# Modulation vectors: full-precision matmuls tile by tile, or split float32r tiles four at a time

## What is computed

```python
sil_c = jax.nn.silu(c)
sil_cc = jax.nn.silu(c_ctx)
mx = (sil_c @ w_ada[l] + b_ada[l])[:, None, :]      # w_ada[l]: 1024 x 6144, float32
mc = sil_cc @ w_ada[l] + b_ada[l]
xsh1, xsc1, xg1, xsh2, xsc2, xg2 = jnp.split(mx, 6, axis=-1)
csh1, csc1, cg1, csh2, csc2, cg2 = jnp.split(mc, 6, axis=-1)
px = _split_in(_modulate(x, xsh1, xsc1) @ w_in[l])  # _modulate: x * (1 + scale) + shift
pc = _split_in(_modulate(ctx, csh1, csc1) @ w_in[l])
```

## Time and profile before

| what | us |
|---|---|
| median of 3 runs (4956.92 to 4962.1) | 4957.29 |
| the profiled execution | 4959.43 |
| its span in the trace | 4957.7 |
| TensorE busy, whole span | 4444.5 |
| VectorE busy | 2856.5 |
| ScalarE busy | 1816.6 |
| modulation matmuls (line 676), 768 records, busy | 88.9 |
| first row copied (line 657) | 25.77 |
| last row copied | 103.15 |
| bias added (line 692) | 107.02 |
| first matmul of the mixers | 133.67 |

### The profile page before, as it was taken

The page is one execution under the profiler, slowest core; times in us unless marked ns, Lnnn a source line. Parts: engine busy times, 40 slices in busy tenths (PEclk is TensorE's granted clock), DMA queues, the critical chain, the costliest instruction groups (busy, mean ns, idle before and its releaser), DMA issues. The chain is left out here.

```text
span 4957.7 us, 59869 instructions
## 1 busy us (share of the span) xinstructions
PE 4444.5 (90%) x22171; PEld 3705.2 (75%) x22171; DVE 2856.5 (58%) x5083; ACT 1816.6 (37%) x2570; POOL 413.2 (8%) x308
## 2 busy tenths in 40 slices
PE   7888888877998556999999996999999999899998
PEld 5777775654874355999999995776878877677887
DVE  1577776775445987888888885334343333344332
ACT  1546554333321033333333332346233233643322
POOL 0000000000001611222222220000000000000000
PEclk9899999998999788999999998999999999999999
DMA  6111111102321025878787782211323322122232
GB/s 247 64 39 35 39 35 34 47 17 70 91 93 49 22 102 222 281 269 281 270 279 274 276 279 80 73 56 39 98 90 98 96 75 68 41 72 92 94 96 83
DMA packets 195952, 578.14 MB, mean 117 GB/s; under 512 B 17328, under 2 KB 66736, under 8 KB 194352
## 3 DMA queue, kind: packets, MB, share of 16 engines
q1 hardware_dynamic: 157888, 433.77, 25.9%
q0 software_dynamic: 36864, 134.23, 8.0%
q10 hardware_dynamic: 1008, 7.55, 0.4%
HBM read 548.22 MB, written 27.26 MB: 116 GB/s over the span
## 5 line engine op out<-in xcount | busy, mean ns | idle before, releaser
L402 DVE TENSOR_TENSOR tile_rest<-tile_raw,tile_up 128x1024 fp32r<-128x1024 f32 (+2 forms) x288 | 338.5, 1180 | 782.2 <-ACT tile_up L393 782.1
L410 PE MATMUL layer_psum<-hn_up,tile_up 128*128 128x512 f32 x1344 | 534.8, 398 | 20.8 <-DVE hn_rest L497 20.8
L411 PE MATMUL layer_psum<-hn_up,tile_rest 128*128 128x512 f32 x1344 | 527.1, 392 | 0.0
L412 PE MATMUL layer_psum<-hn_rest,tile_up 128*128 128x512 f32 x1344 | 526.8, 392 | 0.0
L393 ACT ACTIVATE tile_up<-tile_raw 128x1024 fp32r<-128x1024 f32 (+2 forms) x288 | 291.5, 1018 | 369.0 <-PE layer_psum L412 368.2
L2159 PE MATMUL ex_psum<-ex_t_up,ex_u_up 128*128 128x384 f32 x1024 | 344.2, 336 | 11.3 <-ACT ex_prod L2233 6.6
L2177 PE MATMUL ex_psum<-ex_prod_up,ex_v_up 128*128 128x384 f32 x1024 | 342.8, 335 | 2.3 <-DVE xT L2299 2.3
L2160 PE MATMUL ex_psum<-ex_t_up,ex_u_rest 128*128 128x384 f32 x1024 | 343.8, 336 | 0.0
L2161 PE MATMUL ex_psum<-ex_t_rest,ex_u_up 128*128 128x384 f32 x1024 | 343.7, 336 | 0.0
L2179 PE MATMUL ex_psum<-ex_prod_rest,ex_v_up 128*128 128x384 f32 x1024 | 342.7, 335 | 0.0
L2178 PE MATMUL ex_psum<-ex_prod_up,ex_v_rest 128*128 128x384 f32 x1024 | 342.6, 335 | 0.0
(11 more groups left out here) (440 smaller groups left out, 10145.2 us busy)
## 6 DMA issues: line engine op xcount, KB each, us to landing
ex_u<-in_peer_u SPq DMA_DIRECT2D x128, 512.0 KB, 6.5
tT<-in_peer_v SPq DMA_DIRECT2D x128, 512.0 KB, 7.0
tile_raw<-in_w_gu SPq DMA_DIRECT2D x88, 512.0 KB, 3.6
xT<-in_w_head SPq DMA_DIRECT2D x56, 512.0 KB, 3.6
mod_w<-in_w_ada SPq DMA_DIRECT2D x48, 512.0 KB, 4.7
mg_w_raw<-in_w_merge SPq DMA_DIRECT2D x48, 512.0 KB, 3.6
expert_table<-et_rows SPq DMA_DIRECT2D x6, 4096.0 KB, 11.8
ex_rows<-expert_table SPq DMA_DIRECT2D x64, 384.0 KB, 7.9
```

The lines of the kernel that those rows point to most:

```text
L402: self.nc.vector.tensor_tensor(out=self.rest[:, n % self.SLOTS, 0:blocks, :], in0=self.raw[n % self.RAWS][:, 0:blocks, :], in1=self.up[:, ...
L410: self.nc.tensor.matmul(dst, w_up, up, start=first, stop=False)
L411: self.nc.tensor.matmul(dst, w_rest, up, start=False, stop=False)
L412: return self.nc.tensor.matmul(dst, w_up, rest, start=False, stop=last)
```

## The change

The matmuls of the stage are made in float32r with split operands, on four tiles at once. `sil` is cut in two parts that stand beside each other as four stationary columns (`both`: columns 0 and 1 the rounded part, 2 and 3 the remainder). Each weight tile is cut too: ScalarE copies the loaded tile `raw` to `up` (line 678 of the new kernel), VectorE writes `raw - up` to `w_rest` (723). There are six `raw` buffers and two sets of `up` and `w_rest`, a set being four tiles; the `w_rest` sets lie in the still unused `mem.x_up` and `mem.x_rest`. For each of the twelve groups of four tiles TensorE makes 16 matmuls of 512 moving columns: for each d one against `up` and one against `w_rest` (705, 706). A result has four rows, the parts of the two vectors, and two adds on VectorE (730, 731) bring them together. ScalarE copies a group's rows (670) into one of two small row buffers, and TensorE transposes them in fours (694) one group behind instead of all 48 at the end. A load buffer is free again when VectorE has cut its tile. TensorE waits for all of ScalarE's loads at its start. The loops over six columns of tiles are written out.

```diff
+    GROUP = 4
+    GROUPS = 6 * DB // GROUP
+    RAWS = 6
...
         def _(sp):
-            with sp.Fori(0, 6) as i:
-                for k in range(8):
-                    load_tile(sp, w, 0, k, i, io["w_ada"][i, k])
+            for n in range(GROUPS * GROUP):
+                if n >= RAWS:
+                    sp.wait_ge(w_cut, START + n - RAWS + 1)
+                sp.dma_start(raw[n % RAWS][:], io["w_ada"][n // 8, n % 8]).then_inc(landed[n % RAWS], 16)
...
-            with act.Fori(0, 6) as i:
-                for half in range(2):
-                    act.wait_ge(w.filled, w.fill_at(0, (half + 1) * PER_BANK - 1, i))
-                    nc.scalar.activation(rows[:, bass.ds(i * D + half * 512, 512)], B[half][0:2, :],
-                                         ACT.Copy).then_inc(row_out, 1)
+            act.wait_ge(sil_ready, START + 1)
+            nc.scalar.activation(both[:, :, 0:2], sil[:], ACT.Copy).then_inc(sil_up_ready, 1)
+
+            def row(g):
+                act.wait_ge(filled, START + g + 1)
+                if g >= 2:
+                    act.wait_ge(turned, START + g - 1)
+                nc.scalar.activation(rows[:, g % 2, :], B[g % 2][0:4, :], ACT.Copy).then_inc(row_out, 1)
+
+            for g in range(GROUPS):
+                for k in range(GROUP):
+                    n = g * GROUP + k
+                    act.wait_ge(landed[n % RAWS], START + 16 * (n // RAWS + 1))
+                    if g >= 2:
+                        act.wait_ge(filled, START + g - 1)
+                    nc.scalar.activation(up[g % 2][:, k, :, :], raw[n % RAWS][:], ACT.Copy).then_inc(w_up_ready, 1)
+                    if k == 1 and g > 0:
+                        row(g - 1)
+            row(GROUPS - 1)
...
-                    for d in range(DB):
-                        last = nc.tensor.matmul(B[half][0:2, at * P:(at + 1) * P], sil[:, d, :], w.ring[k][:, d, :],
-                                                start=d == 0, stop=d == DB - 1)
-                    last.then_inc(w.filled, 1)
...
+            def turn(g):
+                pe.wait_ge(row_out, START + g + 1)
+                for k in range(GROUP):
+                    m = g * GROUP + k
+                    last = nc.tensor.transpose(B[2][:, 4 * m:4 * m + 4], rows[:, g % 2, k * P:(k + 1) * P],
+                                               mem.c("ident")[0:4, 0:4])
+                last.then_inc(turned, 1)
+
+            pe.wait_ge(sil_cut, START + 1)
             pe.wait_ge(x_loaded, START + 64)
...
+            for g in range(GROUPS):
+                pe.wait_ge(w_cut, START + (g + 1) * GROUP)
+                if g >= 2:
+                    pe.wait_ge(row_out, START + g - 1)
+                for d in range(DB):
+                    nc.tensor.matmul(B[g % 2][0:4, :], both[:, d, :], up[g % 2][:, :, d, :], start=d == 0, stop=False)
+                    last = nc.tensor.matmul(B[g % 2][0:4, :], both[:, d, :], w_rest[g % 2][:, :, d, :], start=False,
+                                            stop=d == DB - 1)
+                last.then_inc(filled, 1)
+                if g > 0:
+                    turn(g - 1)
+            turn(GROUPS - 1)
...
+            for n in range(GROUPS * GROUP):
+                g, k = n // GROUP, n % GROUP
+                dve.wait_ge(w_up_ready, START + n + 1)
+                if g >= 2:
+                    dve.wait_ge(filled, START + g - 1)
+                nc.vector.tensor_tensor(out=w_rest[g % 2][:, k, :, :], in0=raw[n % RAWS][:],
+                                        in1=up[g % 2][:, k, :, :].bitcast(F32), op=ALU.subtract).then_inc(w_cut, 1)
...
+            seq(nc.vector.tensor_tensor(out=mem.mod[:], in0=sums[:, :, 0, :], in1=bias, op=ALU.add))
+            seq(nc.vector.tensor_tensor(out=mem.mod[:], in0=sums[:, :, 1, :], in1=mem.mod[:], op=ALU.add))
```

More of the change, by code:

```diff
@@ L620, in phase_modulation @@
 def phase_modulation(nc, io, mem):
-    PER_BANK = 512 // P
+    GROUP = 4
+    GROUPS = 6 * DB // GROUP
+    RAWS = 6
     with Phase(nc, "mod") as ph:
-        w = ph.stream(8, [(6, 8, list(range(8)))])
         B = ph.banks()
         cond, sil = ph.sb("cond", [P, DB, 2]), ph.sb("sil", [P, DB, 2])
+        both = ph.sb("both", [P, DB, 4], F32R)
+        raw = [ph.sb(f"raw{n}", [P, DB, P]) for n in range(RAWS)]
+        up = [ph.sb(f"up{g}", [P, GROUP, DB, P], F32R) for g in range(2)]
+        w_rest = [t[:].rearrange("p d t -> p (d t)").rearrange("p (k d n) -> p k d n", k=GROUP, d=DB)
+                for t in (mem.x_up, mem.x_rest)]
         masks = ph.sb("masks", [P, N_MASKS, P])
-        rows = ph.sb("rows", [2, 6 * D])
+        rows = ph.sb("rows", [4, 2, GROUP * P])
+        landed = [ph.sem(f"landed{n}") for n in range(RAWS)]
+        w_up_ready, w_cut, filled = ph.sem("w_up_ready"), ph.sem("w_cut"), ph.sem("filled")
+        sil_up_ready, sil_cut = ph.sem("sil_up_ready"), ph.sem("sil_cut")
         x, cm = mem.attT, mem.convT[:, 0:4, :].rearrange("p b t -> p (b t)").rearrange("p (d c) -> p d c", c=C)
@@ L634, in phase_modulation @@
         order, modulated, up_ready, cut = ph.sem("order"), ph.sem("modulated"), ph.sem("up_ready"), ph.sem("cut")
-        w.credited.append(row_out)
-        block = ph.block(w)
+        block = ph.block()
         @block.sync
         def _(sp):
-            with sp.Fori(0, 6) as i:
-                for k in range(8):
-                    load_tile(sp, w, 0, k, i, io["w_ada"][i, k])
+            for n in range(GROUPS * GROUP):
+                if n >= RAWS:
+                    sp.wait_ge(w_cut, START + n - RAWS + 1)
+                sp.dma_start(raw[n % RAWS][:], io["w_ada"][n // 8, n % 8]).then_inc(landed[n % RAWS], 16)
         @block.scalar
@@ L679, in _ @@
-            pe.wait_ge(row_out, START + CREDIT + 12)
-            pe.wait_ge(x_loaded, START + 64)
[L681 to L684, removed]
+            def turn(g):
[5 more added lines that the diff above has]
+                last.then_inc(turned, 1)
@@ L686, in _ @@
+            turn(GROUPS - 1)
         @block.vector
         def _(dve):
+            dve.wait_ge(sil_up_ready, START + 1)
+            nc.vector.tensor_tensor(out=both[:, :, 2:4], in0=sil[:], in1=both[:, :, 0:2].bitcast(F32),
+                                    op=ALU.subtract).then_inc(sil_cut, 1)
+            for n in range(GROUPS * GROUP):
[5 more added lines that the diff above has]
+                                        in1=up[g % 2][:, k, :, :].bitcast(F32), op=ALU.subtract).then_inc(w_cut, 1)
@@ L688, in _ @@
             seq = Order(dve, order)
-            seq.body(0, 2)
-            dve.wait_ge(turned, START + 1)
+            seq.body(0, 3)
+            dve.wait_ge(turned, START + GROUPS)
             bias = mem.par[:, PARAM_AT["b_ada"]].unsqueeze(2).to_broadcast([P, 48, 2])
-            seq(nc.vector.tensor_tensor(out=mem.mod[:], in0=B[2][:, 0:96].rearrange("p (m c) -> p m c", c=2),
-                                        in1=bias, op=ALU.add))
+            sums = B[2][:, 0:192].rearrange("p (m s c) -> p m s c", s=2, c=2)
```

## The result

The changed kernel takes 4997.6 us (median of 6 runs, 4994.78 to 5002.14) against 4957.54 us: ratio 1.0079, interval 1.0066 to 1.0092, some 40 us slower. The forecast was 4991 us with a range of 4969 to 5006 us. The profiled execution took 5002.14 us, its span 5000.0 us.

A forecast was written before the change was run, and what follows sets the result against it. TensorE was taken to bound the opening stage. First row at 31.6 us, eleven periods of 9.8 us and the tail move the `+ 1.0` by 33.7 us: 4957.3 + 33.7 = 4991 us, range 4969 to 5006 us.

The forecast's parts named there:

- The bound: TensorE bounds the opening weight-tile stage, nothing later runs beside it; its end shifts everything behind it, by +33.7 us.
- The ring: From one ScalarE row copy to the next: pause 4.0 us with two cuts per engine, plus burst; 9.8 us.
- The matmuls: A group's 16 float32r matmuls of 512 columns start 0.23 us apart at full clock, 0.43 us at half.
- The clock: Behind each pause TensorE runs 4.1 us at half clock, 9.6 matmuls slow; a group's burst of matmuls takes 5.8 us.
- rival 3: Clock never comes back inside a group's burst: 7.1 us, period 11.1 us, 5006 us; chance 0.11, shared with dearer matmuls.
- Start and tail: First matmul at 25.3 us, first row at 31.6, twelfth at 139.4; `+ 1.0` at 141.0 instead of 107.3 us.
- Rival 1: TensorE's clock holds at 1.00 in every group: period 7.9 us, +12.8 us, 4970 us; chance 0.12.
- rival 2: TensorE's matmuls with four stationary columns are cheaper than the mixers'; at 0.066 us spacing 4938 us; chance 0.09.

The follow-up runs named there:

- e1: Changed kernel with ScalarE's row copy of the previous group behind the fourth cut instead of the second; 4943.4 us, ratio 0.9970.
- e3: Changed kernel with ScalarE's row copy behind the third cut of the next group instead of the second; 4965.5 us, ratio 1.0010.
- e4: Changed kernel with ScalarE's row copy behind the first cut of the next group instead of the second; 4998.7 us, ratio 1.0081.
- e2: Changed kernel with 14 matmuls on constants behind each group's transposes, filling TensorE's pause; 4972.4 us, ratio 1.0029.
- e6: e4 with its pause filled by 19 matmuls on constants; 4984.0 us, ratio 1.0053.
- e5: e1 with x, ctx and masks loaded by SyncE behind the 48 weight tiles, TensorE waiting at its start only for constants; 4934.4 us, ratio 0.9951.
- e8: e5 with eight load buffers instead of six; 4934.6 us, ratio 0.9957.

## Why the prediction was right

**The bound.** That the stage stands alone and moves everything behind it held: +39.5 us at its end, some 39 us in the time.

**The ring.** Pause forecast at 4.0 us, measured 3.98 us. The step that decided was reading ScalarE's list: the copy waits for the last group's matmuls, and two cuts of the next stand behind it. e1, e3 and e4 move only this. Their pauses follow it (2.84, 3.98 and 5.11 us with one, two and three cuts, forecast 2.9, 4.0 and 5.2), and in e1, with none, seven of the twelve copies have no wait at all.

**The matmuls.** 0.23 and 0.43 us apart, as in the mixers. The Trainium skill's page "TensorE: Matmul & The Clock Gate" (section "Back-to-back issue gap") gives about 131 ns for matmuls of 512 columns in a real stream. The trace does not agree: e2, with the clock at full, has 0.23 us.

**The clock.** The direction was right, the size is the term that was off. I took 4.1 us at half clock for a burst, a mean of four stretches behind single pauses, and so 9.6 slow matmuls; the trace has twelve (5.1 us) in each of the rings. Burst 6.3 us instead of 5.8, ring 10.24 instead of 9.8: 4.9 of the 5.8 us by which the sum fell short. A small part of it is the reading: the stretches of the earlier trace rows begin about 0.3 us behind the first matmul. Taken from that matmul itself the same four read 0.51, 0.75, 0.77 and 0.50, which makes 4.4 us at half clock. The weak point is one that I named and did not price: those pauses stood behind long activity. Taken singly, the four rows (0.52 to 0.79) stand for 2.5 to 5.8 us at half clock, and the loop settled at 5.1 us in every ring. That the mean of such scattered values came within 1.0 us of it is in part luck. The Trainium skill ("TensorE: Matmul & The Clock Gate", section "HAM oscillation — how this bites in real kernels") describes a kernel in which the wait between bursts makes every burst start at half clock. The trace of the changed kernel agrees in that each of its twelve bursts starts slow. A burst slow from end to end, rival 3, did not occur: the last four matmuls were back at 0.23 us.

**Start and tail.** The first matmul came at 26.08 us, released by the masks, for 25.3 us: their load was issued at 5.30 us instead of 4.99 and took 20.7 us instead of 20.3. Its burst was 6.3 us as forecast. This 0.8 us is the rest of the shortfall (32.41 for 31.6). The tail of 1.67 us instead of 4.16 was as forecast: the transposes in fours were worth 2.5 us.

**The rivals.** Rival 1's full clock came only where the pauses were filled (e2, e6); with shorter ones it held in most bursts (e3, e1). e2 ended at 4972.4 us, 2 us from the 4970 that rival 1 gave for its case. The cheap matmuls of rival 2 showed nowhere. e1 shows what the change gives when the cuts stand beside the matmuls. The argument against rival 3 was weaker than I took it: the 6 us from the matmul at 668.87 us read 0.50, half clock throughout.

## What to carry to other kernels

Write down the ring before judging an overlap: from an engine's wait, through everything that stands behind it in that engine's list, back to the same wait. An instruction in the wrong place of the list (here a copy of 0.59 us) puts all that follows it into the pause of the engine that it waits for. Changing `k == 1` to `k == 3` turned a loss of some 40 us into a gain of 15.

A faster TensorE stage with pauses may run at half clock; what it saves must be computed at the clock it will get, and filling the pause with matmuls on constants is a way to measure that share (25 us here).

## What the runs showed that was not expected

The changed kernel and e4 have pauses of 3.98 and 5.11 us and the same period of 10.24 us, in all eleven rings of both. The slow part of the burst shrank by as much as the pause grew (twelve slow matmuls, then six). With the clock held by filling, the same two pauses give 7.86 and 9.0 us (e2, e6). In e3, with a pause of 2.84 us, the clock stayed at 1.00 for rings of 6.74 us, then fell for two rings and came back, while the pause stayed the same. In e1 it fell inside a burst behind 2.08 us of idle time. So these runs give no length of pause that by itself decides the clock. Equal periods with unlike pauses suggest that the coming and going of the clock sets the period there, and not the sum of the work; that is not shown, and what fixes it at 10.24 us is open: no run varied the pause finely enough.

With all 16 DMA engines shown as busy, the transfers moved 370 GB/s with six buffers (e5) and 395 with eight (e8), against 418 in the opening of the kernel before: a busy share of 1.00 did not mean that the rate was at its end.
